# Hybrid decoder trunk on one core: vector and pool engines share the first norms, beginnings of stages are moved, high parts of the first y features live elsewhere, the scan is written out, the feed-forward opens feature tile by feature tile

## The chip, the core and the metric

One core of one Trainium2 chip. The metric is the device time of one execution in microseconds (us); lower is better. TensorE (PE) is reported with its granted clock, 1.00 for 2.4 GHz and 0.50 for 1.2 GHz. The other engines are VectorE (DVE), ScalarE (ACT), GpSimd (POOL) and SyncE (SP, which here only starts DMAs).

## What is computed

One sequence of 512 tokens, width 1024, float32, goes through two layers. The inputs are made with jax.random and reference() is plain jax.

```python
for i in range(DEPTH):              # DEPTH = 2
    hn = rms_norm(h, mix_norm_w[i])
    mix = nsa_mixer(hn, ...) if i % 2 == 0 else ssd_mixer(hn, ...)
    h = h + mix
    h = h + swiglu(rms_norm(h, ffn_norm_w[i]), w_gate[i], w_up[i], w_down[i])
```

`nsa_mixer` is sparse attention: 16 query heads in 4 groups, head width 64. Queries and two kinds of keys are RMS-normed per head and turned by rotary position (partial: 16 of 64 columns); a third pair of keys and values is compressed from blocks of 32 tokens by a small two-layer network; with 512 tokens all blocks are selected, so the selected and the window branch are both causal attention over everything, each with its own keys. Gates mix the three outputs, then comes `w_out`. `ssd_mixer` is Mamba-2: a projection to z, x, B, C and dt, a convolution over 4 tokens, and a scan over 4 chunks of 128 tokens in each of 4 groups (`y_diag + y_off`, a state carried on), then `y * silu(z)`, an RMS norm per group and `w_out`. `swiglu` has a hidden width of 2816.

## The kernel before

Every engine has its own hand-written instruction list; semaphores order them, and nothing is scheduled by a planner. `trunk` holds all of it, as one block per engine (`block.tensor`, `block.scalar`, `block.vector`, `block.gpsimd`, `block.sync`).

**Split products.** A float32 product is made of three reduced-precision ones: weights and activations are split into a high and a low part (`wh`/`wl`, `xh`/`xl`, `hh`/`hl`, `yh`/`yl`), and `split_product` (L453 to L455) multiplies high by high, high by low and low by high. Weights come in 111 chunks of 128x2048 through a ring of two raw buffers. For each chunk SP starts the load, ACT casts the high part (`split_hi`, L1048), DVE subtracts for the low part (`split_lo`, L1465), and PE waits for `lo_done`. For activations ACT makes `xh` (`x_hi`, L1062) and DVE `xl` (`x_lo`, L1475). In `chunk_F` PE takes the two output tiles of a chunk one after the other, each over all its feature tiles; `chunk_T` gives token-major output.

**Beginning.** SP loads `cols`, then eight tiles of x with four quarters of the first weight chunk between them. PE warms up with six matmuls on zeros (L605), then waits for the low parts of quarter 0 and tile 0. ACT squares the tiles one by one and POOL adds them up (L2029) for the first norm.

**Attention lead-in.** After the products for group 0, ACT copies `proj` and squares it into `qn`. DVE sums per head (L1768), POOL takes the power -0.5 (L2055) and then norms and turns token tile after token tile (`qk_norm`: L2064, L2065, L2071 to L2074, and the copy L2076): all four tiles for group 0. PE meanwhile multiplies the compression blocks (L653), then transposes `hid_rows` (L836) and, once all four tiles are normed, heads 0 to 2 (L663). It then makes the compressed keys (L842) and values (L846), transposes heads 3 to 5, then the normed compressed key (L850), and enters 64 steps of attention (`step_of_attention`, S = 0 to 63, and four more to drain). ACT and DVE make high and low parts of what was transposed (L1201; L1644 and L1646). A step of PE does scores (`qk`, L680 to L690), transposed probabilities of three steps before (`pT`, L743), in groups 0 to 2 pieces of the next group's projection (`project`, L783), and, at fixed places, transposes (L705), compressed scores (L716, L724, L731) and products with values (`pv`, L759 and L763). In group 3 there is no next group; `out_early(t)` puts the output projection's first six feature tiles into every second step, at the step's end. Feature tiles 6 and 7 follow after the loop.

**Scan.** After the convolution PE makes z in two weight chunks (`chunk_T`, banks `FIRST_Z_BANKS`); between them stand the running sums of dt*A (L923), and in the second chunk the transpose of these sums (L1018). The sums go to DRAM and come back broadcast as `rowc`; ACT makes differences and exponentials (`decays`: L1347, L1353), POOL the inputs and `Lx*cbm` (`inputs`: L2124 to L2132), DVE states and outputs, and PE `y` (L1004) out of them. `group(g, last)` is called by `scan_groups`: group 0, a hardware loop over groups 1 and 2, and group 3. PE fills groups 0 to 2 with pieces of the next z (L954). Group 3 has no next z: there it is filled with the first half of the Mamba output projection (feature tiles 0 to 7), by `half_product(t)` for output tile t at the places in `FILL_AT`. Its operands `yh` (L1396) and `yl` (L1917) can only be made in group 3, because `yh` lies over `xh` and `xl`, which z reads until the end of group 2. After the scan feature tiles 8 to 15 follow; then x is split again (L1062, L1475) and the second feed-forward begins with `chunk_F`.

```python
def group(g, last):                    # PE, in outline, for chunk k of 4
    ...
    z_at(0)                            # z pieces, or half_product in the last group
    ...                                # state products, y products (L995, L998, L1004)
    z_at(1)
    if k or not isinstance(g, int) or g:
        to_features(g, k - 1)          # transposes of the normed y (L938): waits y_scaled
    z_at(2)
```

## Time and profile before

| | |
|---|---|
| median of 3 runs | 1496.41 us (1496.11 to 1498.18) |
| the profiled execution | 1497.67 us, its span 1495.9 us |
| PE busy | 1466.1 us, 98% |
| DVE, ACT, POOL busy | 814.8, 616.3, 256.5 us |
| mean granted clock of PE | 0.990 |
| DMA | 139.17 MB, mean 93 GB/s |

Busy time of an engine is the time in which it has at least one instruction under way; matmuls overlap, so a PE that is busy 98% is one that is never without work for long, and a matmul of 512 columns starts every 0.23 us although it is shown as 0.39 us long. The rest of the profile says when PE had nothing under way, what it waited for, and at which clock it ran.

### The profile page before, as it was taken

How to read it: one execution, taken by the hardware profiler on the slowest of the kernel's cores; microseconds unless marked ns; L12 is line 12 of the kernel's file. 1: busy time of each engine (PE TensorE's matmuls, PEld its weight loads, DVE VectorE, ACT ScalarE, POOL GpSimd, SP SyncE). 2: the span in 40 equal slices, each digit the busy share in tenths (PEclk: the TensorE clock that was granted, in tenths of full speed). 3: DMA queues.
4: the chain of work that ended last, by engine and by line, in shares of the span. 5: the costliest groups of instructions: out<-in, count | busy, mean ns of one | idle time of the engine just before them, and what ended most of it. 6: DMA issues, size and time to landing. Idle time of an engine off the chain costs nothing.

```text
span 1495.9 us, 19967 instructions
## 1 busy us (share of the span) xinstructions
PE 1466.1 (98%) x7418; PEld 1200.5 (80%) x7418; DVE 814.8 (54%) x1091; ACT 616.3 (41%) x997; POOL 256.5 (17%) x292
## 2 busy tenths in 40 slices
PE   9989999999999999999999999998999999999999
PEld 7868888777888888888888877777887888888887
DVE  4657766865444444332487745778544645444222
ACT  6457666754432222232233356678324322232221
POOL 4333334100300000010000007675203000000000
PEclk9989999999999999999999999999999999999999
DMA  8200010211222222233232233332222222323222
GB/s 333 86 29 29 29 58 1 113 57 57 90 107 93 103 89 107 88 110 112 85 113 85 84 115 112 113 112 85 85 85 85 99 98 84 112 84 112 100 98 84
DMA packets 23341, 139.17 MB, mean 93 GB/s; under 512 B 2672, under 2 KB 3440, under 8 KB 8944
## 3 DMA queue, kind: packets, MB, share of 16 engines
q1 hardware_dynamic: 20688, 127.80, 23.9%
q10 hardware_dynamic: 2592, 10.55, 2.0%
q8 instruction: 39, 0.64, 0.2%
q14 instruction: 22, 0.18, 0.0%
HBM read 136.18 MB, written 2.16 MB: 92 GB/s over the span
## 4 chain that ended last, share of the span: by engine, by line
PE 86%; DVE 4%; POOL 4%; issue 4%; ACT 2%; POOLq 0%; DVEq 0%; ACTq 0%
PE ps L453 23%; PE ps L455 22%; PE ps L454 22%; PE ps L783 5%; PE ps L954 3%; PE ps L763 2%; PE ps L743 2%; DVE wl L1465 1%; PE ps L1004 1%; POOL Lx L2132 1%; PE ps L687 1%; PE ps L688 1%; POOL sqacc L2029 1%; PE ps L759 1%; PE ps L716 1%
## 5 line engine op out<-in xcount | busy, mean ns | idle before, releaser
L1465 DVE TENSOR_TENSOR wl<-wraw,wh 128x2048 fp32r<-128x2048 f32 x111 | 257.1, 2316 | 251.0 <-ACT wh L1048 251.0
L453 PE MATMUL ps<-xh,wh 128*128 128x512 f32 (+2 forms) x912 | 358.2, 393 | 2.4 <-DVE xl L1475 1.7
L455 PE MATMUL ps<-xh,wl 128*128 128x512 f32 (+2 forms) x912 | 355.2, 389 | 0.0
L454 PE MATMUL ps<-xl,wh 128*128 128x512 f32 (+2 forms) x912 | 355.0, 389 | 0.0
L1048 ACT ACTIVATE wh<-wraw 128x2048 fp32r<-128x2048 f32 x111 | 211.8, 1908 | 182.8 <-PE ps L455 182.6
L453 PEld LDWEIGHTS ps<-xh,wh 128*128 128x128 f32 (+2 forms) x912 | 170.1, 186 | 40.0 <-issue 2.8
L455 PEld LDWEIGHTS ps<-xh,wl 128*128 128x128 f32 (+2 forms) x912 | 170.0, 186 | 37.5
L454 PEld LDWEIGHTS ps<-xl,wh 128*128 128x128 f32 (+2 forms) x912 | 170.1, 187 | 36.4 <-issue 0.7
L453 PE MATMUL ps<-hh,wh 128*128 128x512 f32 x352 | 136.9, 389 | 0.0
L454 PE MATMUL ps<-hl,wh 128*128 128x512 f32 x352 | 136.9, 389 | 0.0
L455 PE MATMUL ps<-hh,wl 128*128 128x512 f32 x352 | 136.9, 389 | 0.0
L2029 POOL TENSOR_TENSOR sqacc<-sqacc,sq 128x512 f32<-128x512 f32 x32 | 46.3, 1446 | 427.1 <-ACT sq L1057 424.4
L1118 ACT ACTIVATE hh<-hid 128x512 f32 (+1 forms) x44 | 27.8, 632 | 173.9 <-DVE hid L1552 173.9
L1113 ACT ACTIVATE gate<-gate 128x512 f32<-128x512 f32 x44 | 27.7, 633 | 138.9 <-DVE gate L1544 138.9
L1703 DVE TENSOR_REDUCE sm<-ps 128x2 f32<-128x256 f32 (+3 forms) x64 | 52.7, 823 | 48.6 <-PE ps L690 31.5
L455 PEld LDWEIGHTS ps<-hh,wl 128*128 128x128 f32 x352 | 66.1, 188 | 13.8
L454 PEld LDWEIGHTS ps<-hl,wh 128*128 128x128 f32 x352 | 66.1, 188 | 13.8
L453 PEld LDWEIGHTS ps<-hh,wh 128*128 128x128 f32 x352 | 66.1, 188 | 13.5
L1231 ACT ACTIVATE PT<-ps 128x256 f32<-128x256 f32 (+3 forms) x64 | 45.1, 705 | 76.9 <-PE ps L743 76.8
L1223 ACT ACTIVATE Pm<-ps,sm 128x128 f32<-128x128 f32 (+3 forms) x128 | 66.3, 526 | 10.3 <-DVE sm L1703 9.2
L1544 DVE TENSOR_TENSOR gate<-ps,tmp 128x512 f32<-128x512 f32 x44 | 29.9, 688 | 71.0 <-PE ps L455 71.0
L1835 DVE SCALAR_TENSOR_TENSOR tmp<-raw,cols,tmp 128x511 f32<-128x511 f32 (+2 forms) x72 | 54.0, 750 | 8.6 <-DVE tmp L1835 1.5
(285 smaller groups left out, 2381.0 us busy)
## 6 DMA issues: line engine op xcount, KB each, us to landing
wraw<-wstream SPq DMA_DIRECT2D x111, 1024.0 KB, 4.7
rowc<-cum_rows ACTq DMA_DIRECT2D x16, 512.0 KB, 3.6
cw<-cw_in SPq DMA_DIRECT2D x1, 4096.0 KB, 14.0
xT<-xT_in SPq DMA_DIRECT2D x8, 256.0 KB, 6.4
part<-xT_in ACTq DMA_DIRECT2D x1, 2048.0 KB, 10.4
out<-xT SPq DMA_DIRECT2D x8, 256.0 KB, 6.5
wraw<-wstream SPq DMA_DIRECT2D x4, 256.0 KB, 5.4
wraw<-wstream SPq DMA_DIRECT2D x2, 512.0 KB, 8.4
```

Of the source, the lines that this page charges most:

```text
L453: mm(o, wa[0], xa[0], start=start, stop=False)
L454: mm(o, wa[0], xa[1], start=False, stop=False)
L455: return mm(o, wa[1], xa[0], start=False, stop=stop)
L783: ins = mm(ps[:, 7, :], (xh, xl, xh)[pss][:, kt, t], (wh, wh, wl)[pss][:, slot, w], start=m == 0, stop=m == 23)
L954: ins = mm(ps[:, z_bank_of(tt), :], (xh, xl, xh)[pss][:, kt, t], (wh, wh, wl)[pss][:, slot, w], start=m == 0, stop=m == 23)
L1048: A(wh[:, n % 2, :], wraw[:, n % 2, :], ACT.Copy).then_inc(hi_done, 1)
L1223: A(Pm[:, S % LAG, b, 0:w], src, ACT.Exp, bias=sm[:, 4, m + b:m + 1 + b], accum_out=sm[:, 4, m + 4 + b:m + 5 + b]).then_inc(expd, 1)
L1231: A(probsT(i)[:, h % 2], ps[:, 4:6, 0:(i + 1) * P].rearrange("p b (j q) -> p b j q", q=P), ACT.Copy).then_inc(pT_done, 1)
L1465: TTo(wl[:, s, :], wraw[:, s, :], wh[:, s, :].bitcast(F32), ALU.subtract).then_inc(lo_done, 1)
L1703: dve.tensor_reduce(sm[:, 4, m:m + 2], src.rearrange("p (b n) -> p b n", b=2) if i < 2 else src, AX, ALU.max, negate=True).then_inc(negmax, 1)
L1835: ins = STT(out=c[:, d:], in0=x[:, 0:SEQ - d], scalar=w(3 - d), in1=c[:, d:], op0=ALU.mult, op1=ALU.add)
L2029: TTo(sqacc[:, :], sqacc[:, :], sq[:, mt % 2, :], ALU.add).then_inc(acc_done, 1)
```

## The change

The change touches each of the parts above.

1. **Beginning.** SP loads tile 0 of x ahead of `cols`; ACT's queue loads the first weight quarter. PE warms up with four matmuls, and takes feature tile 0 in three sweeps (high by high for all token tiles, then with the low x, then with the low weights), each after its own wait. ACT makes `split_hi(3)` before, not behind, the four copies of `kvc`.
2. **Shared norms.** For group 0 POOL norms token tiles 0 and 1, DVE tiles 2 and 3 (with `Pm` as scratch). DVE's `split_lo(6)` and the gates come after that.
3. **Attention lead-in.** PE transposes all six heads first, then makes compressed keys, then values (in another bank). Norm, transpose and split of the compressed key move into steps 1 to 3 of the attention loop.
4. **End of attention.** `out_early` stands ahead of the transposes, compressed parts and products with values of its step (but for t = 0); of feature tiles 6 and 7 the first four output tiles take tile 6 before PE waits for tile 7.
5. **Scan lead-in.** The sums L923 stand ahead of the last token tile of the first z chunk, their transpose ahead of the first token tile of the second, the first chunk products ahead of its last.
6. **High parts of y.** `yh` is cut into `yh0`, `yh2` (over parts of `BCf` that are read by then), `yh4` and `yh10` (over `xh` and `xl`, but for the first two tiles of each). Feature tiles 0 to 3 are split in groups 1 and 2, and `FILL_AT` puts the output projection's first half, for tiles 0 and 1, into pieces: with feature tiles 0 to 3 in chunk 0 of group 3, with tiles 4 to 7 in chunk 1.
7. **Scan written out.** `scan_groups` calls `group` four times with constants; there is no hardware loop.
8. **Feed-forward.** The first chunk of each feed-forward goes over feature tiles outside and the two output tiles inside (`first_chunk`). Before the second one, tiles 0 and 1 of x are split while the last output products still run.

```diff
+OLD_KT, NEW_KT, FIRST_KTS = range(4), range(4, FIRST_KT), range(FIRST_KT)
+FILL_AT = {(0, 1): ((0, OLD_KT),), (0, 2): ((1, OLD_KT),), (1, 0): ((0, NEW_KT),), (1, 2): ((1, NEW_KT),),
+           (2, 0): ((2, FIRST_KTS),), (2, 2): ((3, FIRST_KTS),), (3, 0): ((4, FIRST_KTS),), (3, 2): ((5, FIRST_KTS),)}
...
-        yh = a.take("yh", [P, TT, 16, P], F32R)
+        a.end += 2 * SEQ * 4
+        yh4 = a.take("yh4", [P, TT, 6, P], F32R)
+        a.end += 2 * SEQ * 4
+        yh10 = a.take("yh10", [P, TT, 6, P], F32R)
+        a = Region(bc_at)
+        yh0 = a.take("yh0", [P, TT, 2, P], F32R)
+        a = Region(bc_at + SG * SEQ * 4)
+        yh2 = a.take("yh2", [P, TT, 2, P], F32R)
...
+            def first_chunk(n, L):
+                pe.wait_ge(lo_done, n + 1)
+                s = n % 2
+                for kt in range(KT):
+                    fresh(L)(kt)
+                    for m in range(2):
+                        w = slice(kt * 256 + m * P, kt * 256 + (m + 1) * P)
+                        ins = split_product(ps[:, 4 + m, :], (wh[:, s, w], wl[:, s, w]), xs(kt), kt == 0, kt == KT - 1)
...
                 if LAG <= S < STEPS + LAG:
                     pT(S - LAG)
+                early = S - (STEPS - HP * TT) - 5
+                if early > 0 and early % 2 == 0:
+                    out_early(early // 2)
                 if round_at(S):
                     turn_keys_queries(*round_at(S))
...
+                if S == 2:
+                    pe.wait_ge(kcn_done, 1)
+                    pe.transpose(ps[:, 6, 3 * P:4 * P], kcn[:, :, :].rearrange("p a d -> p (a d)"), ident[:, :]
+                                 ).then_inc(kcT, 1)
...
             def z_bank(tt):
                 if tt == 3:
+                    pe.wait_ge(dt_done, 1)
+                    for k in range(3):
+                        ins = mm(ps[:, 6, k * P:(k + 1) * P], tri[:, k, :], dtb[:, 1, :], start=True, stop=True)
+                    ins.then_inc(cum_mm, 1)
                     pe.wait_ge(featT_done, 16)
...
+                    if (g, k) == (SG - 3, 2):
+                        act.wait_ge(yT_done, TT)
+                        rows_hi(0)
+                    if (g, k) == (SG - 2, 1):
+                        rows_hi(2)
...
+            dve.wait_ge(qk_rstd, TT)
+            dve.wait_ge(sincos_done, 2)
+            for tt in range(POOL_TILES, TT):
+                q6 = qn[:, tt, :, 0, :]
+                step(TTo(q6, proj[:, tt, 0:6, :], sm0[:, 2, tt, :].unsqueeze(2).broadcast_to([P, 6, DH]), ALU.mult))
+                step(TTo(q6, q6, rows[:, ROW_W6:ROW_W6 + 384].rearrange("p (h d) -> p h d", d=DH), ALU.mult))
...
+                dve.tensor_copy(qn[:, tt, :, 1, :], q6).then_inc(qk_normed, 1)
+            split_lo(6)
             dve.wait_ge(gates_exp, 1)
...
+                    if (g, k) == (SG - 2, 1):
+                        y_lo(1, TT, slice(0, TT), slice(0, 2))
+                    if (g, k) == (SG - 2, 2):
+                        y_lo(2, TT, slice(0, TT), slice(2, 4))
```

What the lines do to the order of the instructions is shown at two places. The first is DVE between the first norms' sums (`sm_68<-qn`) and the first scores' maxima (L1703). Before, with the gates (`glin`), a weight split (L1465) and the whole chain of the compressed key (`kcn`):

```order
L1772 TENSOR_SCALAR sm_68<-sm_68 128x18
L1774 TENSOR_SCALAR glin<-glin 128x192
L1775 RECIPROCAL glin<-glin 128x192
L1777 TENSOR_TENSOR glin<-glin,cmask 128x64
L1644 TENSOR_TENSOR qA<-ps,qA 64x512 x3
L1465 TENSOR_TENSOR wl<-wraw,wh 128x2048
L1782 TENSOR_REDUCE stat<-kcn 128x1
```

In the changed kernel (its own line numbers):

```order
L1847 TENSOR_SCALAR sm_68<-sm_68 128x18
L1852 TENSOR_TENSOR qn<-proj,sm_68 128x6x64
L1853 TENSOR_TENSOR qn<-qn,rows 128x6x64
...
L1861 COPY qn<-qn 128x6x64
L1540 TENSOR_TENSOR wl<-wraw,wh 128x2048
L1864 TENSOR_SCALAR glin<-glin 128x192
L1865 RECIPROCAL glin<-glin 128x192
L1867 TENSOR_TENSOR glin<-glin,cmask 128x64
L1719 TENSOR_TENSOR qA<-ps,qA 64x512 x4
L1721 TENSOR_TENSOR kB_94<-ps,kB_95 128x512 x2
```

Two token tiles of seven instructions each now stand in front, the weight split and the gates follow, and the low parts of the transposed heads (`qA`, `kB`) come as one run behind them.

The second place is PE at the beginning of scan group 3. Before, chunk 0 holds its own products (L998, L1004), then the transposes of `ybuf` and the next chunk products, and only then the first output product:

```order
L998 MATMUL ps<-xdd,btst 128x512
L1004 MATMUL ps<-xdt,Lx 128x64 x8
L938 MATMUL ps<-ident,ybuf 128x128 x4
L930 MATMUL ps<-bc 128x128
L931 MATMUL ps<-ident,bc 128x128
L453 MATMUL ps<-yh,wh 128x512
L454 MATMUL ps<-yl,wh 128x512
```

In the changed kernel:

```order
L1058 MATMUL ps<-xdd,btst 128x512
L1064 MATMUL ps<-xdt,Lx 128x64 x8
L472 MATMUL ps<-yh_134,wh 128x512
L473 MATMUL ps<-yl,wh 128x512
L474 MATMUL ps<-yh_134,wl 128x512
...
L996 MATMUL ps<-ident,ybuf 128x128 x4
L472 MATMUL ps<-yh_134,wh 128x512
L473 MATMUL ps<-yl,wh 128x512
L474 MATMUL ps<-yh_134,wl 128x512
```

Twelve output products (feature tiles 0 to 3 of output tile 0; `yh_134` and `yh_135` are `yh0` and `yh2`) now stand between the chunk's own products and the transposes of `ybuf`, and twelve more behind these.

## Rows read from the trace of the kernel before

**Rows 1.** The page: engines' busy time; DVE's weight splits (busy, mean ns | idle before).

```profile
PE 1466.1 (98%) x7418; PEld 1200.5 (80%) x7418; DVE 814.8 (54%) x1091; ACT 616.3 (41%) x997; POOL 256.5 (17%) x292
...
L1465 DVE TENSOR_TENSOR wl<-wraw,wh 128x2048 fp32r<-128x2048 f32 x111 | 257.1, 2316 | 251.0 <-ACT wh L1048 251.0
```

**Rows 2.** Waits of PE: us in total, times, longest us.

```profile
PE ps L938 <- DVE ybuf L1904: 3.0, 2, 1.9
PE ps L954 <- DVE wl L1465: 2.8, 2, 1.4
...
PE ps L1004 <- POOL Lx L2132: 1.8, 1, 1.8
PE ps L453 <- DVE xl L1475: 1.7, 1, 1.7
PE ps L731 <- DVE pc L1695: 1.3, 1, 1.3
PE ps L759 <- ACT PT L1231: 1.1, 1, 1.1
...
PE ps L453 <- DVE yl L1917: 0.9, 1, 0.9
PE ps L930 <- DVE btst L1895: 0.7, 1, 0.7
```

**Rows 3.** Stretches of 20 us: length, PE, PEld, DVE, ACT, POOL busy, PEclk, DMA share, GB/s.

```profile
80.00:100.00 20.00, 17.12 (x76) 15.00 (x77) 12.41 (x31) 8.34 (x22) 2.48 (x7) 0.68 0.16 54
...
300.00:320.00 20.00, 18.05 (x112) 14.14 (x109) 10.92 (x25) 9.16 (x23) 0.00 (x0) 0.91 0.17 54
...
400.00:420.00 20.00, 20.00 (x90) 16.54 (x89) 12.83 (x15) 7.37 (x8) 0.00 (x0) 1.00 0.19 59
...
900.00:920.00 20.00, 19.23 (x86) 15.71 (x87) 9.66 (x13) 13.03 (x30) 16.01 (x13) 0.83 0.48 159
...
1020.00:1040.00 20.00, 16.10 (x75) 12.39 (x74) 19.43 (x21) 18.63 (x34) 11.34 (x10) 0.83 0.33 111
```

**Rows 4.** Timeline, first 31 us: start, length, engine, line, what, idle before.

```profile
11.42 0.63 ACT L1136 ACTIVATE wh<-wraw 128x512 fp32r<-128x512 f32 x1 [0.90 <-DMA wraw<-wstream]
15.45 13.22 POOL L2029 TENSOR_TENSOR sqacc<-sqacc,sq 128x512 f32<-128x512 f32 x8 [13.77 <-ACT sq L1057]
```

**Rows 5.** Timeline, attention lead-in.

```profile
65.53 3.22 POOL L2055 TENSOR_TENSOR sm<-sm,mhalf 128x18 f32<-128x18 f32 x1
67.55 1.35 DVE L1775 RECIPROCAL glin<-glin 128x192 f32<-128x192 f32 x1
68.83 0.83 POOL L2064 TENSOR_TENSOR qn<-proj,sm 128x384 f32<-128x384 f32 x1
68.94 0.82 DVE L1777 TENSOR_TENSOR glin<-glin,cmask 128x64 f32<-128x64 f32 x1
80.47 2.82 PE L663 MATMUL ps<-ident,qn 128*128 128x128 f32 x12 [4.41 <-POOL qn L2076]
83.83 3.62 PE L846 MATMUL ps<-cw,hidV 128*128 128x64 f32 x16
91.00 1.29 DVE L1646 TENSOR_TENSOR kB<-ps,kB 128x512 fp32r<-128x512 f32 x2
92.44 0.36 PE L680 MATMUL ps<-kB,qA 128*128 128x256 f32 x1 [1.81 <-DVE kB L1646]
```

**Rows 6.** Timeline, scan lead-in.

```profile
881.33 0.29 DVE L1882 SCALAR_TENSOR_TENSOR dtb<-dtb 128x128 f32<-128x128 f32 x1
884.49 0.83 PE L923 MATMUL ps<-dtb,tri 128*128 128x128 f32 x6
897.35 4.47 POOL L2132 TENSOR_TENSOR Lx<-Lx,cbm 128x512 f32<-128x512 f32 x2 [7.98 <-DVE btst L1895]
```

**Rows 7.** Timeline, beginning of scan group 3.

```profile
1023.72 8.49 DVE L1917 TENSOR_TENSOR yl<-yT,yh 128x1024 fp32r<-128x1024 f32 x4
1038.97 0.66 PE L938 MATMUL ps<-ident,ybuf 128*128 128x128 f32 x4 [1.07 <-DVE ybuf L1904]
```

More of the change, by code:

```diff
@@ L355, in after, with scan_groups @@
                 engine.wait_ge(semaphore, value)
-        def scan_groups(engine, group, enter=None, leave=None):
-            group(0, False)
-            with engine.Fori(0, SG - 2) as i:
-                if enter:
-                    enter(i)
-                group(i + 1, False)
-            if leave:
-                leave()
-            group(SG - 1, True)
+        def scan_groups(group):
+            for g in range(SG):
+                group(g, g == SG - 1)
         Q4 = "p (h d) -> p h d"
@@ L1394, in group @@
                         act.wait_ge(yT_done, 2 * TT)
-                        for kt in range(0, FIRST_KT, 2):
-                            A(yh[:, :, kt:kt + 2, :], yT[:, :, kt:kt + 2, :], ACT.Copy).then_inc(yh_done, 1)
+                        rows_hi(4)
+                        rows_hi(6)
                     if last and k >= 2:
@@ L1442, in _ @@
             split_hi(n0 + 1)
-            for c in range(3):
-                split_hi(n0 + 2 + c)
-            act.wait_ge(products, 2 * (n0 + 4))
+            split_hi(n0 + 2)
+            split_hi(n0 + 3)
             for kt in range(KT):
+                if kt == 2:
+                    split_hi(n0 + 4)
+                    act.wait_ge(products, 2 * (n0 + 4))
                 act.wait_ge(evac, t0 + kt + 1)
@@ L1981, in _ @@
             split_lo(n0 + 2)
-            scan_groups(dve, group, lambda i: V.enter(i, DVE_SCAN_STEPS), lambda: V.leave(SG - 2, DVE_SCAN_STEPS))
+            scan_groups(group)
             y_mean_square(SG - 1, 3)
@@ L2000, in _ @@
                     split_lo(n0 + 2 + c)
-            for kt in range(KT):
+                if c == 2:
+                    x_lo(NORM["ssm_out"], 0)
+                    x_lo(NORM["ssm_out"], 1)
+            for kt in range(2, KT):
                 x_lo(NORM["ssm_out"], kt)
```

233 lines of the change are left out of this document (144 added, 89 removed).

## The prediction

> **What bounds the kernel now.** I read the page first, then PE's waits, then stretches of 20 us for the clock, then the timeline around each long wait. The page says that PE is busy 1466.1 of 1495.9 us and every other engine at most 54% [rows 1]. PE's work is hardly changed by the diff (two warm-up matmuls fewer), so time can only come from what PE loses. It loses in two ways. The first is waiting, 29.8 us in all; the longest are 13.3 us [rows 2] and, in the attention lead-in, 4.4 and 1.8 [rows 5]. They lie in five places: attention lead-in, end of attention, scan lead-in, scan groups and second feed-forward. The second does not show as idle: PE's clock falls to its lower level (1.2 GHz) behind clusters of such waits. A stretch of 20 us at 0.68 holds 2 x 0.32 x 20 = 12.8 us at the lower level, one at 0.91 holds 3.6, and the two at 0.83 hold 6.8 each [rows 3]: 30 us. Work at half clock takes twice as long, so a busy PE loses half of them, up to 15 us. Both losses together, some 45 us, are the ceiling of what any reordering can give. Elsewhere 90 matmuls start in 20 us with no gap [rows 3], about 0.23 us each; 12 of them (one output tile over four feature tiles) take 2.7 us.
>
> **Beginning.** Tile 0 of x and the first weight quarter come one DMA issue or more earlier, and the first sweep no longer waits for the low parts. But what follows is paced by the fourth weight quarter, which ACT takes at 11.42 straight from its DMA, and by POOL's eight additions from 15.45 to 28.67, which start behind ACT's work on that quarter and on the last tiles of x [rows 4]. The bytes ahead of them are the same. A PE that starts 1 us earlier mostly waits later. I take -0.4 us here and -0.3 for the earlier `split_hi(3)`; ends 0 and -1.5. Two warm-ups fewer can leave the first matmuls at the lower clock; there is a microsecond of slack for that.
>
> **Attention lead-in.** PE waits 4.4 us for POOL's four tiles, until 80.47, and enters the loop at 92.44, behind another wait of 1.8 [rows 5]. In the changed kernel the powers are ready at 68.75 as before. POOL then needs one more tile, DVE two. POOL's first product of a tile takes 0.83 us [rows 5], its tile 3.9 (a quarter of the way from 68.83 to 80.4, three tiles). DVE's seven instructions per tile are an estimate: two of 384 columns and the copy at 0.5 us, four small ones at 0.2, four semaphore steps of 0.1: 2.6 us, two tiles 5.2, so done at 74.0, if both engines run freely. They don't: DVE's product of 64 columns (`glin`) took 0.82 us beside POOL's product and ended 0.1 us behind it (69.76 against 69.66) [rows 5]. So I add POOL's 3 us of products to DVE's time: 77.0. PE is free at 80.47 - 4.41 = 76.1, so its wait of 4.4 becomes 1.
>
> The Trainium skill ("SBUF — State Buffer", section "Who interferes with whom") has this as a rule: a VectorE instruction with two SBUF inputs and a GpSimd one that reads SBUF exclude each other for the whole instruction. The row agrees. With the engines free the heads would be ready 3 us earlier, at 82, and PE's own path would decide, so this part would give some 2 us more; by the rule it is as taken.
>
> From 77.0 PE needs, at the lower clock, 24 transposes at 2.82/12 (5.6 us), keys 0.9 and values 3.6 [rows 5]: 87; at the full clock half of that: 82. DVE is late in another way: weight split 2.3 us [rows 1], gates 2.0 (the reciprocal 1.35 [rows 5], two small ones), then six low parts in a row at 0.65 [rows 5], 3.9 us, so heads are ready at 85.2 instead of 92.4, whatever PE does. Between 85.2 and 87 I take 85.4: -7.0 us. The first 3 to 4 us of the loop were at the lower clock; PE is now steadier and I count half of that stretch back, -1.4. Against it, PE now waits in step 2 for the compressed key, whose 1.4 us on DVE now stand behind the maxima: +0.6. Sum -7.8; ends -4 (DVE's tiles one after the other with POOL's, clock low through the loop's start) and -11.
>
> **End of attention.** `out_early(2)`, 18 matmuls or 4.1 us, now stands ahead of the transposes of `pc` (wait 1.3), `out_early(7)` ahead of the last `pv` (wait 1.1) [rows 2]; both cover more than the wait. The price would be a later `o_copy` at the very end; there the 12 matmuls on feature tile 6 (2.7 us) stand ahead of the wait for tile 7 (ACT 0.6, DVE 0.7). The clock's fall at 304, 3.6 us [rows 3], came behind the 1.3 and should go: -1.8. Sum -4.2; ends -2.4 and -4.4.
>
> **Scan lead-in.** dt*A is ready at 881.62; L923 runs at 884.49 [rows 6] and can now run at 884.49 - 2.7 = 881.8, just in time. Sums, row store, row loads, decays and POOL's `Lx` all follow from it, 2.7 us earlier; so do the first chunk products. The waits of 0.7 and 1.8 (L930, L1004) [rows 2] shrink to some 0.3, and the fall of the clock behind them (6.8 us [rows 3]) should go: -3.4. New: PE reaches the second z chunk before DVE has split it, whose split comes 2.7 us earlier too, about +0.6. POOL's two `Lx` products took 4.47 us [rows 6] beside a weight split, and that pair stays. Sum -2.2 - 3.4 + 0.6 = -5.0; ends -2.5 and -6.
>
> **Scan group 3.** Before, PE waited 1.9 (L938) and 0.9 (`yl`) in a row, then the clock fell for 6.8 us, and then 1.1 at 1038.97 [rows 2, 3, 7]: 3.9 + 3.4 = 7.3 us. Now two pieces of 2.7 us need only what groups 1 and 2 prepared, and cover the first two waits. DVE has two low parts instead of four here (8.49 us [rows 7] becomes 4.3) and is free 4 us earlier. But PE comes 5 to 6 us earlier, so DVE's next weight split and scaling make it wait about 2 us where it waited 1.1, and some 1 us in chunk 2. Sum -4.8; ends -2 (clock falls again) and -7. The two high and low parts moved into groups 1 and 2 stand where DVE and ACT have idle time within a chunk; POOL's products there had some 3 us of slack. If not, PE's waits for L1465 at the group boundaries (2.8 in two [rows 2]) grow; otherwise they stay, since the same chain of DVE instructions makes them.
>
> **Scan written out** removes register and branch instructions that PE doesn't wait for: 0, ends +-1. **Feed-forward.** The wait for `xl` of 1.7 us [rows 2] is covered by tiles 0 and 1, and each further tile gives PE 1.4 us of work for 0.7 of preparation: -1.7; ends -0.5 and -1.8.
>
> **Sum.** -0.7 - 7.8 - 4.2 - 5.0 - 4.8 + 0 - 1.7 = -24.2 us. The profiled execution took 1497.67 us, so 1473.5 in its terms; it lies 1.3 us above the median of the runs, so **1472.2** on the median.
>
> **Rivals.**
> - *DVE becomes the pace.* Heads stay late, and in the last scan group DVE (19.43 of 20 us busy [rows 3]) sets the time, so the two largest terms shrink to their ends: +3.8 and +2.8, and the lead-in of the scan to -2.5: 1472.2 + 9 = 1481. For it speaks the row of DVE blocked by POOL. Against it, DVE's work in that stretch falls by 4 us.
> - *The clock doesn't come back.* All waits go as forecast but the clock falls at the same places, because new waits stand there: 1.4 + 1.8 + 3.4 + 3.4 = 10 us less: 1482. A smaller form of it: the lead-in now has 24 transposes in one run; in the trace 12 of them took 2.82 us, twice the length of those in the loop, so they ran at the lower level. If it stays there, PE enters the loop at 87 and not 85.4, and the -1.4 goes: 1475, at 0.3 within the forecast's own chance. The Trainium skill ("TensorE: Matmul & The Clock Gate", section "Part 4: PE-mode transpose") says that transposes don't keep the clock up as other matmuls do, which would make this form the rule; the row agrees and doesn't prove it.
> - *It goes better.* All terms at their far ends: -31.7, 1465.
> - *Slower.* Written-out scan groups mean that PE, ACT, DVE and POOL fetch new instructions where the loop repeated old ones. If that held up PE, the 4 groups' some 650 matmuls would need over 24/650 = 0.04 us more each to eat the gain. The attention's 64 steps are written out already and PE is 20.00 of 20 us busy in much of them. Price from that point on: 1500.
> - *No effect.* Each wait covered uncovers another one equally long, because ACT, DVE and POOL are in truth the pace: 1496. PE's 98% speak against it.
>
> **How the numbers follow.** Forecast, with its neighbours from 1467 to 1477: 0.55. DVE the pace: 0.14. Clock: 0.13. Better: 0.11. No effect 0.03, slower 0.04. About 0.2% (3 us) is what a measurement of this kernel tells from no change. Faster by more than that 0.94, within it 0.03, slower 0.03. The range has to reach the rivals at 1481 and 1482 and most of the better case: 1464 to 1483.
>
> **What would show it.** PE's first transposes (`qn`) should start near 77 and the first scores near 85, with DVE's last `kB` low part just ahead; if they start below 82, DVE and POOL didn't disturb each other. No wait for `pc` and `PT` at the end of attention; L923's counterpart 2.7 us earlier against the z chunk; `y` of the first scan chunk with under 0.5 us of wait; in group 3 one wait of 1 to 2.5 us for `ybuf` and none for `yl`; clock 0.83 gone from both scan stretches and 0.91 from 300 to 320. The forecast is wrong if PE's waits still sum to over 20 us, or if the mean clock stays at 0.990.

## Result and profile after

The changed kernel takes 1471.57 us (median of four runs, 1469.91 to 1473.84) against 1496.7 us for the kernel before in the same session: ratio 0.9832, 95% interval 0.9813 to 0.985. The forecast was 1472.2. The profiled execution took 1473.84 us, its span 1472.0; in those terms the forecast was 1473.5.

The page of the changed kernel, engines' busy time, as in [rows 1]:

```profile
PE 1453.8 (99%) x7414; PEld 1190.6 (81%) x7414; DVE 821.5 (56%) x1106; ACT 614.2 (42%) x998; POOL 250.6 (17%) x278
```

PE's busy time fell by 12.3 us and its idle time from 29.8 to 18.2 us: 23.9 together, the whole difference of the spans. Of the 12.3, 1.9 are the two warm-ups; the other 10.4 are about what the clock gave back. Summed over stretches of 20 us, (1 - PEclk) x 20 comes to 15.4 us before and 5.4 after.

Waits of PE in the changed kernel (us in total, times, longest), as in [rows 2]:

```profile
PE ps L1012 <- DVE wl L1540: 3.2, 3, 1.5
PE ps L649 <- ACT wh L1198: 2.7, 1, 2.7
PE ps L725 <- DVE kB L1721: 1.9, 1, 1.9
...
PE ps L996 <- DVE ybuf L2008: 1.1, 1, 1.1
```

Gone from the list are the 4.4 us for POOL's `qn`, the waits for `kcn`, `Lx` (but for 0.13), `btst`, `pc`, `xl` and `yl`, and the last one for `PT`. L649, the first real product, is new with 2.7 us. L1012 is the former L954: 2.8 in two, and the 0.24 that the earlier sums bring. Stretches, columns as in [rows 3]:

```profile
0.00:20.00 20.00, 16.19 (x57) 12.87 (x58) 11.66 (x15) 13.20 (x20) 5.96 (x10) 0.91 0.86 301
80.00:100.00 20.00, 18.01 (x95) 14.03 (x94) 14.67 (x44) 12.31 (x38) 4.02 (x8) 0.91 0.06 25
300.00:320.00 20.00, 20.00 (x169) 15.94 (x165) 10.35 (x18) 9.22 (x23) 0.00 (x0) 1.00 0.30 106
...
900.00:920.00 20.00, 20.00 (x108) 16.15 (x107) 12.49 (x22) 11.88 (x29) 13.87 (x13) 1.00 0.15 53
1000.00:1020.00 20.00, 18.38 (x97) 14.60 (x96) 19.10 (x23) 18.61 (x35) 12.28 (x11) 0.95 0.38 131
1020.00:1040.00 20.00, 20.00 (x95) 16.20 (x94) 16.71 (x18) 10.84 (x21) 9.79 (x9) 0.96 0.16 54
```

The fall of [rows 3] at 80 us has shrunk from 0.68 to 0.91, those at 300 and 900 are gone, that at 1020 has shrunk. One at the very beginning is new.

To see where the time left, I put the same piece of work in both traces side by side. Each term is the shift that its stretch adds:

| mark | before | after | shift | term | forecast | measured |
|---|---|---|---|---|---|---|
| compression products begin | 61.17 | 61.37 | +0.2 | beginning | -0.7 | +0.2 |
| ACT issues `part` in the attention | 279.1 | 270.5 | -8.6 | attention lead-in | -7.8 | -8.8 |
| transposes of dt | 873.1 | 859.9 | -13.2 | end of attention | -4.2 | -4.6 |
| z product after its wait, group 1 | 947.90 | 929.47 | -18.4 | scan lead-in | -5.0 | -5.2 |
| the same, group 2 | 987.41 | 968.84 | -18.6 | groups 1, 2 | 0 | -0.1 |
| last product | 1491.8 | 1467.6 | -24.2 | group 3 and FFN | -6.5 | -5.6 |

The last output product (1129.5 before, 1107.2 after) parts the last row: group 3 has 3.7 of it, the second feed-forward 1.95. That the sum of -24.2 was met to the tenth is luck: the terms are each up to 1 us off, and the beginning's error was paid by the lead-in's.

Timeline of the changed kernel, attention lead-in (start, length, engine, line, what, idle before; DVE's rows first, then ACT's, then PE's), to be read against [rows 5]:

```profile
68.36 0.56 DVE L1852 TENSOR_TENSOR qn<-proj,sm 128x384 f32<-128x384 f32 x1 [3.40 <-POOL sm L2169]
...
71.85 0.48 DVE L1861 COPY qn<-qn 128x384 f32<-128x384 f32 x1
72.25 0.64 DVE L1852 TENSOR_TENSOR qn<-proj,sm 128x384 f32<-128x384 f32 x1
...
74.53 0.36 DVE L1861 COPY qn<-qn 128x384 f32<-128x384 f32 x1
74.80 2.29 DVE L1540 TENSOR_TENSOR wl<-wraw,wh 128x2048 fp32r<-128x2048 f32 x1
...
79.38 2.52 DVE L1719 TENSOR_TENSOR qA<-ps,qA 64x512 fp32r<-64x512 f32 x4 [0.45 <-ACT qA L1263]
81.93 1.29 DVE L1721 TENSOR_TENSOR kB<-ps,kB 128x512 fp32r<-128x512 f32 x2
...
75.78 1.28 ACT L1256 ACT_TABLE_LOAD   x1
...
78.73 2.07 ACT L1263 ACTIVATE qA<-ps 128x512 fp32r<-128x512 f32 x4
...
76.09 1.47 PE L708 MATMUL ps<-ident,qn 128*128 128x128 f32 x12
77.75 1.53 PE L708 MATMUL ps<-ident,qn 128*128 128x128 f32 x12 [0.19 <-ACT hidK L1256]
...
83.36 0.55 PE L725 MATMUL ps<-kB,qA 128*128 128x256 f32 x1 [1.90 <-DVE kB L1721]
```

DVE's two tiles end at 74.9, not 77.0. The first takes 3.97 us beside POOL's, the second, which only the end of POOL's touches, 2.64. PE finds them ready, and its 24 transposes take 3.0 us, not 5.6. Then it waits 1.9 us for DVE's last low part, the one that was forecast to come last, and enters the loop at 83.4 where 85.4 was forecast.

### The profile page after: what moved, and what is told of

It reads as the page before. It is cut to its first block, busy times and chain, and to the rows that moved or that the text cites. A ratio compares the mean times of both kernels' runs of the same rounds, so it can differ in the third digit from the quotient of the medians.

```text
span 1472.0 us, 19641 instructions
## 1 busy us (share of the span) xinstructions
PE 1453.8 (99%) x7414; PEld 1190.6 (81%) x7414; DVE 821.5 (56%) x1106; ACT 614.2 (42%) x998; POOL 250.6 (17%) x278
## 4 chain that ended last, share of the span: by engine, by line
PE 89%; POOL 3%; DVE 3%; ACT 2%; issue 2%; DMA 0%; ACTq 0%; SPq 0%; POOLq 0%; DVEq 0%
PE ps L472 24%; PE ps L474 23%; PE ps L473 23%; PE ps L828 4%; PE ps L808 2%; PE ps L788 2%; PE ps L1012 2%; POOL Lx L2247 1%; PE ps L698 1%; PE ps L732 1%; PE ps L733 1%; PE ps L1064 1%; PE ps L804 1%; ACT seg L1410 1%; DVE wl L1540 1%
## 5 line engine op out<-in xcount | busy, mean ns | idle before, releaser
L1285 ACT ACTIVATE Pm<-ps,sm 128x128 f32<-128x128 f32 (+3 forms) x128 | 66.2, 526 | 11.6 <-DVE sm L1778 10.6
```

The source lines that it names most:

```text
L1285: A(Pm[:, S % LAG, b, 0:w], src, ACT.Exp, bias=sm[:, 4, m + b:m + 1 + b], accum_out=sm[:, 4, m + 4 + b:m + 5 + b]).then_inc(expd, 1)
```

## Experiments

The base line is the changed kernel in nine runs (four above, five below): 1469.9 to 1475.3, median 1473.2. The kernel before has 1496.3 to 1496.9 in the three sessions. In all tables "idle" is PE's, "clock" the sum of (1 - PEclk) x 20, both of the profiled execution.

### The beginning and the scatter

The changed kernel unchanged (`a_again`): 

> The changed kernel once more, unchanged, as the base line for what follows. Its four times so far lie in two clusters, 1469.9 (twice, mean clock 1.000) and 1473.2 to 1473.8 (clock 0.997). Theory A: they differ by the first real matmuls alone. PE idles 2.7 us between the warm-ups and the first product (4.66 to 7.36) and in the slow cluster then runs 3.5 us at half clock, which costs it some 1.8 us, plus falls elsewhere. Expected: again two clusters some 3.5 us apart. Rival R: the two clusters come from a later place (the clock's fall at 83 or at 1018 us); then the same two clusters, but a profile of the fast cluster has no fall at 83 or 1018 and may keep the one at 8 us.

Six warm-ups (`a_warm6`): 

> Six warm-up matmuls instead of four, all else as changed. They end near 6.5 instead of 4.66, so PE idles 0.9 us instead of 2.7 before its first product at 7.36. Theory A: the clock doesn't fall at 8 us, the slow cluster is gone or rare, all times near 1470, median 1.5 us below the unchanged form. Rival R (later place): same two clusters, median unchanged at 1471.6 within 0.5.

```diff
-            for _ in range(4):
+            for _ in range(6):
                 mm(ps[:, 5, 0:256], qA[:, 0, 0:P].bitcast(F32), qA[:, 0, 0:256].bitcast(F32), start=True, stop=True)
```

Table first as well (`a_cols_warm`): 

> Six warm-ups, and the small table of columns is the first issue of the sync queue again (the first weight quarter stays on ACT's queue). In the changed kernel ACT's first high part waits for that table until 5.97, in the kernel before it began at 4.40. Theory A: ACT's first high part near 4.6 to 5, first product near 6.5, behind the warm-ups' end, 0.8 earlier than 7.36; nothing else paces PE before the column sums (PE arrives there 2.7 us behind POOL's last addition), so all of it is kept: near 1469.2. Rival: the first tile of x lands later by what the table takes and nothing is gained: 1470.

```diff
+            sp.dma_start(cols[:, :], cols_in).then_inc(cols_landed, 16)
             for k in range(KT):
                 sp.dma_start(xT[:, k, :], xT_in[:, k, :]).then_inc(x_landed[k], 16)
-                if k == 0:
-                    sp.dma_start(cols[:, :], cols_in).then_inc(cols_landed, 16)
-                elif k < 4:
+                if 0 < k < 4:
```

The old beginning (`u_begin`): 

> The whole beginning as in the kernel before (table first, first weight quarter by the sync queue, six warm-ups, first feature tile as high-high, low-high, high-low per token tile), except that split_hi(3) stays early. My prediction gave the changed beginning 0.4 us; then this one takes 0.4 more than a fast run of the changed kernel, 1470.3, and never falls into the slow cluster. Theory A, sharper: the changed beginning is worth less than nothing with its four warm-ups (median 1471.6 against 1470 here). If instead the beginning carries the gain, this kernel takes over 1473.

```diff
+            sp.dma_start(cols[:, :], cols_in).then_inc(cols_landed, 16)
...
-            for _ in range(4):
+            for _ in range(6):
...
-            for part in range(3):
...
-            for kt in range(1, 4):
+            for kt in range(4):
...
-            act.dma_start(wraw[:, 0, 0:512], wstream[0][:, 0:512]).then_inc(quarter_landed[0], 16)
```

| kernel | median (range), 5 runs | first product | compression products | idle | clock |
|---|---|---|---|---|---|
| `a_again` | 1474.4 (1470.0 to 1475.3) | 7.19 | 61.16 | 18.4 | 0 |
| `a_warm6` | 1473.0 (1470.9 to 1474.2) | 7.46 | 60.09 | 18.2 | 3.4 |
| `a_cols_warm` | 1472.4 (1471.0 to 1474.8) | 7.43 | 61.46 | 19.0 | 5.2 |
| `u_begin` | 1472.9 (1472.2 to 1474.0) | 6.89 | 60.36 | 17.9 | 1.8 |

The four can't be told apart by their medians. The changed beginning is worth nothing that these runs show, and my 0.4 isn't there; nor do `a_warm6` and `u_begin` lie near 1470, as Theory A wanted. The traces say why. First lines of ACT in the kernel before, then in the changed one:

```profile
4.40 0.72 ACT L1062 ACTIVATE xh<-xT,cols 128x512 fp32r<-128x512 f32 x1 [2.15 <-DMA xT<-xT_in]
```

```profile
5.97 0.72 ACT L1123 ACTIVATE xh<-xT,cols 128x512 fp32r<-128x512 f32 x1 [3.26 <-DMA cols<-cols_in]
6.60 0.61 ACT L1198 ACTIVATE wh<-wraw 128x512 fp32r<-128x512 f32 x1
```

Two queues now bring the table, x and weights at once. The weights are there as soon as ACT asks, but the pair of table and x is complete 1.6 us later. Table first doesn't mend it: in `a_cols_warm` ACT waits until 6.05, for `xT`. With the weight quarter back on the sync queue (`u_begin`) the pair is complete at 4.10. So that expectation failed, and what the earlier issue gives, the later landing takes.

Theory A was half right. There is a loss at the first products, but it is no single fall, and the scatter isn't two clusters. Four things differ from trace to trace. The first shows in a trace of a later experiment (`u_norms`, same four warm-ups), first matmuls:

```profile
1.11 3.78 PE L637 MATMUL ps<-qA 128*128 128x256 f32 x8 [1.11 <-POOL qA L2129]
7.86 2.05 PE L649 MATMUL ps<-wh,xh 128*128 128x512 f32 x4 [2.97 <-ACT wh L1198]
9.70 1.91 PE L649 MATMUL ps<-wh,xl 128*128 128x512 f32 x4
11.41 1.91 PE L649 MATMUL ps<-wl,xh 128*128 128x512 f32 x4
```

Its products start 0.43 us apart until 13.9, twice the usual 0.23, though PEclk reads 1.00 for that stretch. All eight passes of the warm-up ran at that slow pace, and behind the idle time the products go on at it. The compression products then begin at 63.15. In the eight traces with four warm-ups 7 to 14 products are slow, and the compression products begin between 61.2 and 63.2. With six warm-ups none is slow in `a_warm6` and `u_begin` (60.1 and 60.4); `a_cols_warm`, idle for 2.1 us behind its warm-ups, has 8 (61.5). The second is the fall behind the 1.9 us at 83: it came in eight of ten traces with that wait (1.8 or 3.4 us) and not in `a_again` and `u_fill`. The third is the fall in group 3, behind the 1.07 us for `ybuf`: it came in three of the ten traces with the new filling.

The fourth eats what six warm-ups give. PE's wait for the weights of the second z chunk, in the changed kernel and in `a_warm6`:

```profile
890.14 0.50 PE L1012 MATMUL ps<-wh,xh 128*128 128x512 f32 x1 [0.24 <-DVE wl L1540]
```

```profile
890.81 0.50 PE L1012 MATMUL ps<-wh,xh 128*128 128x512 f32 x1 [1.25 <-DVE wl L1540]
```

It is 1.25 in the four kernels with six warm-ups (these three and `best`, below) and at most 0.25 in those with four whose sums stand early. ACT's differences begin 6.3 to 7.1 us after the issue of the sums' row store in the first, 5.1 to 6.0 in the second. Why isn't shown. So `a_warm6` is 1.3 us ahead of the changed kernel's trace at the compression products and loses 1.0 of it here.

Two runs of `a_again` took 1474.6 and 1475.3 at a mean clock of 0.999; a start as in `u_norms`, which the clock doesn't show, would explain them, but they have no trace, so this stays open.

The Trainium skill ("TensorE: Matmul & The Clock Gate", "Part 1: The HAM clock gate (the "warmup" mystery)") says that how many matmuls run slow at a kernel's start differs from run to run. These traces agree: 14 slow products in `u_norms` and 7 in `a_again`, whose beginnings are the same.

### One part undone at a time

POOL norms all tiles (`u_norms`): 

> POOL again norms and rotates all four tiles of q and k of group 0, DVE none; everything else of the attention lead-in stays as changed (transposes of all heads in one run, compressed key moved into the loop). Theory (waits and clock): the transposes start at 80.5 as before instead of 76.1, DVE's weight split and gates lie ahead of them, so the low parts follow the transposes closely and the loop is entered near 87 to 88.5 instead of 83.4: 3.5 to 5 us slower than the changed kernel, about 1476 to 1477 where that one is at 1472. Rival (DVE is the pace of the lead-in, the four tiles hidden): the low parts end where they do now, under 1 us slower.

```diff
-POOL_TILES = 2
+POOL_TILES = 4
```

`out_early` at the step's end (`u_end`): 

> Only out_early goes back from its place behind pT to the end of each step; the order of the last products (feature tile 6 first) stays. Theory: the waits of 1.3 us (pc transposes) and 1.1 us (last pv) come back, and in most runs the clock's fall behind the first of them, 1.8 us: 2.4 to 4.2 slower, near 1475. Rival (no effect, the waits move to where out_early stood): within 1 us of the changed kernel.

```diff
-                early = S - (STEPS - HP * TT) - 5
-                if early > 0 and early % 2 == 0:
-                    out_early(early // 2)
                 if round_at(S):
...
-                if early == 0:
-                    out_early(0)
+                early = S - (STEPS - HP * TT) - 5
+                if early >= 0 and early % 2 == 0:
+                    out_early(early // 2)
```

Sums late again (`u_scanlead`): 

> Cumulative sums again behind the first z chunk, their transpose ahead of token tile 1 of the second, first chunk products behind it. Theory: the waits of 0.7 and 1.8 us return with the fall of the clock behind them (3.4 us): 2.5 to 6 us slower, my term says 5: 1477. Rival (POOL's two Lx products end where they did, they're what the first y waits for): waits unchanged against the changed kernel, within 1 us.

```diff
                 if tt == 3:
-                    pe.wait_ge(dt_done, 1)
...
                     pe.wait_ge(featT_done, 16)
             chunk_T(n0, None, 0, range(4), 512, True, False, before=z_bank, banks=FIRST_Z_BANKS)
+            pe.wait_ge(dt_done, 1)
...
+            pe.wait_ge(cum_exp, 1)
+            chunk_products(0, 0)
             scan_groups(group)
```

Filling as before (`u_fill`): 

> In the last scan group the first two output pieces are again done whole in chunk 1 (eight feature tiles each), nothing ahead of chunk 0's end; the homes of the high parts and the moved low parts stay. Theory: PE stands before the chunk's y and yl as before (1.9 us and some of 0.9), and the clock falls behind it (3.4): 4 to 6 us slower, less what the two low parts moved to groups 1 and 2 still save (DVE has 4.3 us of them here instead of 8.5). Rival (the moved low parts carry the gain, the filling doesn't): under 1.5 us slower.

```diff
-FILL_AT = {(0, 1): ((0, OLD_KT),), (0, 2): ((1, OLD_KT),), (1, 0): ((0, NEW_KT),), (1, 2): ((1, NEW_KT),),
+FILL_AT = {(1, 0): ((0, FIRST_KTS),), (1, 2): ((1, FIRST_KTS),),
```

Filling and the moved high and low parts as before (`u_group3`): 

> The filling of the last scan group undone as in the run before, and with it the high and low parts of y's first four features moved back from groups 1 and 2 into chunk 0 of the last group. u_fill alone lay some 2 us above the changed kernel's median of nine runs (1473.2). Theory: DVE again has 8.5 us of low parts in one piece, PE waits 1.9 and some 0.9 again and the clock falls in more runs than not: 4 to 5 us above the changed kernel, 1477 to 1478, my term of 4.8. Rival (the moved parts cost groups 1 and 2 as much as they save in group 3): no slower than u_fill, 1475.

```diff
+                        rows_hi(0)
+                        rows_hi(2)
                         rows_hi(4)
...
-                    if (g, k) == (SG - 3, 2):
-                        act.wait_ge(yT_done, TT)
-                        rows_hi(0)
-                    if (g, k) == (SG - 2, 1):
-                        rows_hi(2)
...
+                        y_lo(1, 2 * TT, slice(0, TT), slice(0, 2))
+                        y_lo(2, 2 * TT, slice(0, TT), slice(2, 4))
```

Feed-forward as before (`u_ffn`): 

> The first chunk of both feed-forwards by output tile again, and x of feature tiles 0 and 1 ahead of the second one prepared in the old order (ACT's last weight split first, DVE's low parts last). Theory: the wait of 1.7 us for xl at the second feed-forward returns: 1.7 slower than the changed kernel, 0.5 to 1.8, near 1475. Rival (the feature-first order alone moves the wait to a later tile): same as the changed kernel, 1473.

```diff
-                first_chunk(n0, L)
+                chunk_F(n0, None, 0, xs, range(KT), (4, 5), True, True, each=fresh(L))
...
-                if c == 2:
-                    x_lo(NORM["ssm_out"], 0)
-                    x_lo(NORM["ssm_out"], 1)
-            for kt in range(2, KT):
+            for kt in range(KT):
```

| undone | median (range), 4 runs | over 1473.2 | compression products | idle | clock |
|---|---|---|---|---|---|
| `u_norms` | 1478.3 (1475.9 to 1480.2) | 5.1 | 63.15 | 22.0 | 5.2 |
| `u_end` | 1476.8 (1476.2 to 1477.9) | 3.6 | 61.83 | 21.4 | 3.6 |
| `u_scanlead` | 1478.4 (1478.2 to 1479.7) | 5.2 | 61.42 | 21.1 | 7.0 |
| `u_fill` | 1475.0 (1474.0 to 1478.0) | 1.8 | 61.85 | 21.1 | 1.8 |
| `u_group3` | 1478.7 (1477.3 to 1479.0) | 5.5 | 62.56 | 20.2 | 5.2 |
| `u_ffn` | 1476.6 (1475.3 to 1476.9) | 3.4 | 61.44 | 19.7 | 5.2 |

The differences of medians carry the scatter of the start, up to 2 us, so I read each beside its trace. Most of the scatter goes if a stretch is measured between two marks. Lead-in: compression products to ACT's issue of `part`; end of attention: on to the transposes of dt, with the first feed-forward in it; scan lead-in: on to the z product of group 1; group 3: from the z product of group 2 to the last output product; last: on to the last product.

| trace | lead-in | end of attention | scan lead-in | group 3 | last |
|---|---|---|---|---|---|
| before | 217.9 | 594.0 | 74.8 | 142.1 | 362.4 |
| `b_unrolled` (below) | 217.0 | 594.0 | 74.8 | 141.8 | 362.4 |
| changed | 209.1 | 589.4 | 69.6 | 138.4 | 360.4 |
| `a_again` | 207.8 | 589.5 | 69.6 | 137.4 | 360.4 |
| `u_norms` | 213.9 | 589.5 | 69.1 | 138.3 | 360.4 |
| `u_end` | 209.3 | 592.1 | 69.6 | 137.4 | 360.4 |
| `u_scanlead` | 209.1 | 589.5 | 74.8 | 137.5 | 360.4 |
| `u_fill` | 207.8 | 589.5 | 69.6 | 139.4 | 360.4 |
| `u_group3` | 209.3 | 589.5 | 69.6 | 141.8 | 360.4 |
| `u_ffn` | 209.3 | 589.9 | 69.6 | 138.3 | 362.4 |
| `best` (below) | 207.4 | 589.5 | 70.6 | 137.5 | 360.4 |

Each part undone lengthens its own stretch; what else moves is the clock at 83 us (207.8 without the fall, 209.1 with the shorter one) and in group 3 (137.4 without, 138.4 with).

*`u_norms`*, waits of PE and timeline:

```profile
PE ps L708 <- POOL qn L2191: 5.8, 1, 5.8
```

```profile
70.17 2.94 POOL L2178 TENSOR_TENSOR qn<-proj,sm 128x384 f32<-128x384 f32 x1
...
70.12 2.29 DVE L1540 TENSOR_TENSOR wl<-wraw,wh 128x2048 fp32r<-128x2048 f32 x1 [3.40 <-POOL sm L2169]
...
83.88 5.34 PE L708 MATMUL ps<-ident,qn 128*128 128x128 f32 x24 [5.85 <-POOL qn L2191]
```

Its late start (1.8 us) aside, the loop is entered 28.1 us after the compression products began (91.21 - 63.15) against 22.0 in the changed kernel (83.36 - 61.37): 6.1 us. At the end of the lead-in 4.8 of them are left: the clock falls here ahead of the loop and costs 3.4 us (0.83 from 80 to 100), in the changed kernel behind its entry, 1.8 us. So 1.6 of the 4.8 are clock and 3.2 waiting. That DVE is the pace of the lead-in, with the tiles hidden, is refuted.

*`u_end`*: both waits return as expected, 2.6 us by the stretch, and the clock didn't fall behind them this time (1.00 in 280 to 340):

```profile
PE ps L776 <- DVE pc L1768: 1.3, 1, 1.3
PE ps L804 <- ACT PT L1291: 1.1, 1, 1.1
```

*`u_scanlead`*: both waits return, and the clock falls (waits, then a stretch with PE's columns alone):

```profile
PE ps L1065 <- POOL Lx L2247: 1.8, 1, 1.8
...
PE ps L989 <- DVE btst L1999: 0.7, 1, 0.7
```

```profile
880.00:900.00 20.00, 17.35 (x72) 0.83 0.49 178
```

That is 2.5 + 3.4 - 0.2 = 5.7 us by the rows and 5.2 by the stretch, against my term of 5.0.

*`u_fill`, `u_group3`*: with the filling undone PE waits 1.9 us for `ybuf` again (3.0 in two waits against 1.1 in one) and 0.45 in chunk 1, 2.4 us in all. But `yl` makes no wait and the clock stays: 1.8 by the medians, 2.1 by the stretch against `a_again`, where the clock stays too, not my 4 to 6. Only with the low parts moved back too does DVE run 8.5 us of them in a row, and PE meets two waits in close order, with the clock falling behind them. Rows of `u_group3`, PE's columns alone in the last:

```profile
1006.42 8.50 DVE L2020 TENSOR_TENSOR yl<-yT,yh 128x1024 fp32r<-128x1024 f32 x4
...
1006.55 1.12 PE L996 MATMUL ps<-ident,ybuf 128*128 128x128 f32 x4 [1.76 <-DVE ybuf L2005]
1008.62 0.76 PE L472 MATMUL ps<-yh,wh 128*128 128x512 f32 x1 [0.32 <-DVE yl L2020]
```

```profile
1000.00:1020.00 20.00, 17.67 (x80) 0.83 0.23 80
```

By the stretch `u_group3` is as long as the kernel before, 4.5 us over `a_again`. Group 3's gain is thus in two halves, the filling for the wait and the moved low parts for the clock; that the clock's half hangs on the low parts rests on one trace of each, and on the mean clocks of all their runs (0.997 to 0.999 against 0.995 to 0.997). The expectation for `u_group3`, 1477 to 1478, was short by 0.7; its late start (62.56) covers that.

*`u_ffn`*: the 1.7 us for `xl` is back, and the last stretch is 1.95 us longer. Another 0.4 is in the first feed-forward, whose first chunk also goes by output tile again (589.9 against 589.5). Together 2.4 us; what the medians show beyond it (3.4) no stretch shows:

```profile
PE ps L472 <- DVE xl L1548: 1.7, 1, 1.7
```

### Written-out scan alone

`b_unrolled`: 

> The kernel before with one edit: its scan groups written out on all engines instead of a loop over groups 1 and 2. Theory: registers and branches aren't what PE waits for: 1496.3 within 1. Rival (fetching new code costs, or the loop's branch cost): more than 1.5 us away from the kernel before, slower by the first, faster by the second; the second would take that much of the 24 us from my other terms.

```diff
-            group(0, False)
-            with engine.Fori(0, SG - 2) as i:
-                if enter:
-                    enter(i)
-                group(i + 1, False)
-            if leave:
-                leave()
-            group(SG - 1, True)
+            for g in range(SG):
+                group(g, g == SG - 1)
```

1495.65 us (1495.28 to 1497.55, 11 runs) against 1496.85 (15 runs): ratio 0.9996, interval 0.9987 to 1.0005. The written-out scan costs nothing and gives nothing that can be measured. It is what the change needs to name group 2 and 3 in its conditions.

### A version that goes further

`best`: 

> The changed kernel with four more edits. Six warm-ups and the column table first, as in a_cols_warm (1472.4). On ACT a tiny Silu right behind the gates' Exp loads Silu's table while ACT is idle (it idled 6.5 us until 75.38; the load of 1.28 us at 75.78 stood ahead of the high parts, which ran 78.73 to 81.6). On DVE the gates (2 us) move behind the six low parts, or they would hold the low parts where they are. Theory: ACT's high parts decide the end of the lead-in, so they come 1.3 us earlier, low parts too, the loop is entered near 82.0 instead of 83.4, PE's wait for kB falls from 1.9 to 0.6 and the clock falls there less often: 1.3 to 2.5 below a_cols_warm, 1470 to 1471. Rival (DVE's gates are what the softmax of step 0 waits for, so the wait comes back in step 3): loop earlier but no gain, 1472.4.

Beside the two edits of `a_cols_warm`:

```diff
             A(glin[:, :, :], glin[:, :, :], ACT.Exp, scale=-1.0).then_inc(gates_exp, 1)
+            A(stat[:, 40:48], mhalf[:, 0:8], ACT.Silu)
...
             split_lo(6)
-            dve.wait_ge(gates_exp, 1)
...
             transposed_lo(0, (3, 4, 5), lambda h: (3, 7, 4)[h - 3])
+            dve.wait_ge(gates_exp, 1)
...
             dve.wait_ge(gates_done, 1)
```

1471.05 us (1470.32 to 1471.21, 5 runs), ratio to the kernel before 0.9828 (0.9815 to 0.9842); 2.1 below the median of the changed kernel's nine runs, 1.4 below `a_cols_warm`, and with 0.9 us of scatter instead of 5.4. Its fastest run isn't faster than the changed kernel's (1469.9), so what five runs show is the slow executions gone, not a shorter best case. Timeline of ACT, DVE and PE, against the rows of the changed kernel above:

```profile
73.85 0.62 ACT L1256 ACTIVATE hidK<-ps,cols 128x128 f32<-128x128 f32 x2
...
75.63 2.06 ACT L1263 ACTIVATE qA<-ps 128x512 fp32r<-128x512 f32 x4
...
78.81 1.29 DVE L1721 TENSOR_TENSOR kB<-ps,kB 128x512 fp32r<-128x512 f32 x2
80.02 0.25 DVE L1899 TENSOR_SCALAR glin<-glin 128x192 f32<-128x192 f32 x1
...
80.25 0.36 PE L724 MATMUL ps<-kB,qA 128*128 128x256 f32 x1 [1.00 <-DVE kB L1721]
...
83.93 0.50 PE L724 MATMUL ps<-kB,qA 128*128 128x512 f32 x1 [0.88 <-ACT Pm L1285]
```

ACT no longer loads a table ahead of `hidK`, so the loop is entered at 80.25: 3.1 us earlier than in the changed kernel, 1.8 of them from the earlier compression products (59.55). The wait for `kB` is 1.0, and no stretch ahead of the last one has a clock below 1.00. The rival is more than half right: of the 1.3 us 0.88 return as a wait for `Pm`, behind the gates, and against `a_again`, where the clock doesn't fall either, the lead-in is only 0.4 us shorter. What it gains on the other traces (209.1 and more) is the fall that doesn't come. As the start of this kernel is better too, how much each of the four edits gives isn't separated.

## Why the prediction was right, and where it wasn't

The kernel was bound by PE's waits and by the clock behind them, and the change takes most of both away. That reading held: idle time and clock account for 21.6 of 23.9 us (11.6 and 10.0), and each undone part returns in its own stretch. The number is nearer than the terms deserve: errors of opposite sign met, and the median of nine runs, 1473.2, is 1.0 above the forecast where that of the first four was 0.6 below.

- **Beginning, forecast -0.4 and -0.3, measured +0.2.** The step that failed is "tile 0 of x and the first weight quarter come one DMA issue or more earlier". Issued earlier isn't landed earlier: ACT's first high part ran at 5.97 instead of 4.40. So does "there is a microsecond of slack for that": with only four warm-ups 7 to 14 products start 0.43 us apart and cost up to 3 us, and nothing behind takes them in, since PE has no gap until 75.8. The early `split_hi(3)` is worth its 0.3 and more: in `u_begin`, which has the old beginning beside it, the compression products begin at 60.4, against 61.2 before, and 0.3 of that is there already at the first weight split that PE waits for (30.57 against 30.88). In these two traces the column sums begin at 30.82 instead of 29.25; 0.94 of that comes back because PE, later, no longer waits for two weight splits (0.68 at 30.88 and 0.26 at 38.63 before).
- **Attention lead-in, forecast -7.8, measured -8.8.** Mis-sized three times. "So I add POOL's 3 us of products to DVE's time: 77.0" was too careful: the two engines disturb each other only while both run, DVE lost 1.3 us and was ready at 74.9. And "whatever PE does" named only DVE as the pace behind the transposes; ACT's high parts, behind a table load of 1.28 us, hold DVE up as well (0.45 us of waiting at 79.38), which `best` shows. So the loop is entered 9.3 us sooner behind the compression products (22.0 us against 31.3), not 7.0. And "I count half of that stretch back, -1.4" isn't in this trace: from the loop's entry to the mark the kernel before needs 186.6 us, the changed one 187.1, because the clock falls again behind the new 1.9 us; in `a_again`, where it doesn't, 185.8. The wait for the compressed key, +0.6 in the forecast, doesn't appear.
- **End of attention, forecast -4.2, measured -4.6.** As worked out, with 0.4 of the first feed-forward in it: both waits return in `u_end`. The clock's fall with the first of them is in both traces with the old order (before and `b_unrolled`) and not in `u_end`.
- **Scan lead-in, forecast -5.0, measured -5.2.** As worked out; `u_scanlead` gives 5.2 back. The sums run at 868.6, DVE's last row of dt ends at 868.4. The new wait for the second z chunk was 0.24 with four warm-ups and 1.25 with six, forecast 0.6.
- **Group 3, forecast -4.8, measured -3.7.** The forecast's own terms, 7.3 less 2 less 1, give -4.3, not -4.8. PE's wait for `ybuf` was 1.07 and not 2, none for `yl` as forecast, and the expected 1 us in chunk 2 came as 0.55 in chunk 0. But the clock fell behind the 1.07 (1.8 us here, 1.0 by the stretch, since a later wait of 0.57 us then doesn't appear); in `a_again` it didn't, and the term is -4.7. That the "two high and low parts moved into groups 1 and 2 stand where DVE and ACT have idle time" held: the waits at the group boundaries are the same 1.4 to 1.5.
- **Feed-forward, forecast -1.7, measured -1.95** in the second one and -0.4 in the first, which the forecast left out; `u_ffn` brings both back.

Two slips change nothing: DVE's seven instructions add up to 2.7 us, not 2.6, and the chances give 0.93 for faster and 0.04 for slower, not 0.94 and 0.03.

Of the rivals, *DVE becomes the pace* fell with the terms themselves (-8.8 and -3.7 where it gave -4 and -2) and with `u_norms`; *slower by instruction fetch* fell with `b_unrolled`; *the clock doesn't come back* holds in a small part: at the start, at 83 us and in group 3 it still differs from run to run. That this makes most of the scatter of 5 us is my reading of the traces; the slowest runs have none. The rival's smaller form fell. PEclk around the transposes of the changed kernel, stretches with PE's columns alone:

```profile
76.00:78.00 2.00, 1.81 (x16) 1.00 0.00 0
78.00:80.00 2.00, 2.00 (x21) 1.00 0.80 283
80.00:82.00 2.00, 1.46 (x14) 1.00 0.62 250
82.00:83.00 1.00, 0.00 (x0) 0.90 0.00 0
83.00:84.00 1.00, 0.64 (x3) 0.50 0.00 0
84.00:86.00 2.00, 2.00 (x7) 0.50 0.00 0
86.00:88.00 2.00, 2.00 (x12) 0.95 0.00 0
```

The transposes run at the upper level to their end, and it falls during the 1.9 us without work; in `a_again` and `u_fill` it doesn't fall even there. In `u_norms` the same 24 transposes stand behind 5.8 us of waiting and take 5.34 us. So it was the wait that set their level in [rows 5], not what they are. The rule that the prediction cites from the Trainium skill ("TensorE: Matmul & The Clock Gate", "Part 4: PE-mode transpose"), that transposes don't keep the clock up as other matmuls do, shows in no run here while they last, though the stretch of 3.0 us is short. Whether they share in the fall right behind them stays open: the 1.47 us waits ahead of the z products of groups 1 and 2, with products of 512 columns just before, brought a fall in none of the traces.

## What to carry to other kernels

When PE is busy 98%, count the waits and add the time at the lower clock behind them: in this kernel the second gain was nearly as large as the first (10.0 and 11.6 us). A wait of 1 to 2 us that goes may take as much again with it, or nothing: not every such wait brings a fall. A wait that is covered by other work only pays if nothing else of its chain is late, so look at each engine that feeds the next step, table loads among them. Judge such edits by stretches between marks in the traces beside the medians: here one kernel scatters by 5 us, more than most of its parts are worth, while stretches that no fall touches repeat within 0.2 us in nearly all traces.

## What the runs showed of the hardware that I had not expected

- PE can start products at half the pace with a recorded clock of 1.00: in `u_norms` products of 512 columns started 0.43 us apart from 7.86 to 13.9, in `a_warm6` 0.23 apart behind six warm-ups and 1.0 us without work.
- The same wait doesn't always bring the clock down, and a longer one isn't surer: 1.07 us in group 3 did in three of ten traces with the new filling, 1.9 us at 83 in eight of ten, 1.47 us ahead of the z products never.
- A weight quarter on a second queue made the first pair of table and x complete 1.6 us later (5.97 against 4.40), though x was issued 0.45 us earlier; with the quarter back on the first queue (`u_begin`) it was complete at 4.10.
- POOL's product of 384 columns took 0.83 us alone, 1.20 beside DVE's tile of short instructions, and 2.94 beside DVE's weight split of 2.29 us. DVE's own split took no longer. With the last, where POOL waits out the whole split, the Trainium skill's rule ("SBUF — State Buffer", "Who interferes with whom"), that the two engines hold their shared port pair one at a time, agrees; with two chains of short instructions each side lost only 1.0 to 1.3 us of some 4.
